# Stick-breaking attention: sums over later keys as split products, with GpSimd making the high part of softplus

## The chip, the cores and the metric

The kernel runs on one core of a Trainium2 chip. The metric is the device time of one launch, in microseconds (us); lower is better. The engines are TensorE (PE in the profile, its weight loads PEld), VectorE (DVE), ScalarE (ACT), GpSimd (POOL) and SyncE (SP), which issues the weight transfers. Each runs its own instructions in order, and they meet at semaphores.

## The reference

Three blocks follow each other on 256 tokens of width 1024. The third has four layers, each a mixer and a squared-ReLU feed-forward part; the mixers of its layers 0 and 3 are stick-breaking attention, with 16 heads of 64:

```
z = einsum('bhqd,bhkd->bhqk', qb, k) * scale
mask = key_pos[None, :] < q_pos[:, None]
log_beta = log_sigmoid(z)
log_1m_beta = where(mask, log_sigmoid(-z), 0.0)
suffix = cumsum(log_1m_beta, axis=3, reverse=True) - log_1m_beta
weights = where(mask, exp(log_beta + suffix), 0.0)
out = einsum('bhqk,bhkd->bhqd', weights, v)
```

With softplus(z) = -log_sigmoid(-z), the exponent is z minus the sum of softplus over this key and all later keys before the query.

## The kernel before

The program is a list of stages (`network`); every engine runs its own part of each stage in turn. All large products of the kernel are split: a weight or a feature x is written as hi + lo, both of type fp32r, where hi is x rounded and lo = x - hi, and three fp32r products replace one fp32 product. ScalarE makes hi of the weights (`in_hi`, line 325) and VectorE makes lo (`in_lo`, line 332).

Keys lie on the partitions, queries in the columns. One step works on a pair of heads. In each head's PSUM bank there are 384 score columns: 256 for the first 128 keys (all queries) and 128 for the last 128 keys (the later queries); so a pair has 768 elements in each partition. `self.e`, `self.sp` and `self.w` are rings of two for |z| and its logarithm, softplus, and weights. `duo` is a ring of three pairs of banks for the scores.

For a pair i the work goes round the engines in this order:

1. TensorE, `_scores`: fp32 products of keys and queries (lines 1629, 1632), and one fp32r product that adds the mask (line 1635).
2. VectorE, `magnitude` (1721): |z|, from PSUM to SBUF.
3. ScalarE: exp(-|z|) and ln(1 + that) (1700, 1701).
4. VectorE, `softplus` (1714): max(z, 0) + that logarithm.
5. TensorE, `_sums` (1643 to 1645): fp32 products of constant matrices of minus one with softplus, added to the scores in the same bank. A fp32 product stands in the trace as two records.
6. ScalarE: the weights, exp of the bank (1692).
7. TensorE, `_values` (1655): fp32 products with the values. ScalarE (1696) and VectorE (1732) then split the result into feat_hi and feat_lo for the output projection.

The eight pairs are pipelined. TensorE's step s is `_scores(s)`, `_sums(s-1)`, `_values(s-2)`. VectorE's step s is `softplus(s-1)`, `magnitude(s)`, then line 1732 for pair s-3. ScalarE's is the weights of s-2, line 1696 for s-3, and lines 1700 and 1701 for s. Steps 0 and 1 stand inside the projection before (`QkvIn`), each after a half of its blocks 4 and 5; there `softplus(0)` comes right before an `in_lo`. Steps 2 to 10 stand in `StickBreaking`. After step LATE = 4 ScalarE and VectorE split one unit of the output projection's weights (`in_hi`, `in_lo`), and `softplus(4)` is behind that `in_lo`. GpSimd has nothing to do in this stage. The output projection (`Linear`, lines 1257 to 1259) begins after the last `_values`.

Of the kernel before, what the change touches and what calls it, by code (L numbers as in the profile page):

```python
# [14 lines left out]
P = 128  # L15
# [121 lines left out]
class Core:  # L137


    def __init__(self, nc, ctx, dram):  # L140
# [49 lines left out]
        self.before_r = placed("before_r", at, F32R, 2, P)  # L190
        self.ident_r = placed("ident_r", at + 4 * 2 * P, F32R, P)
        self.mask_r = placed("mask_r", at + 4 * 3 * P, F32R, 3 * P)
        self.feat2_hi = placed("feat2_hi", at, F32R, KC, TOKENS)
        self.feat2_lo = placed("feat2_lo", at + 4 * KC * TOKENS, F32R, KC, TOKENS)
        self.duo = [ctx.enter_context(nc.psum_tensor(f"duo{i}", [P, 2, 512], F32)) for i in range(4)]
# [90 lines left out]
class Stage:  # L286
# [21 lines left out]
    def gpsimd(self, pool):  # L308
        pass
# [1275 lines left out]
class StickBreaking(Stage):  # L1585
# [12 lines left out]
    def __init__(self, core, before, qT, kT, v, at):  # L1598
        super().__init__(core, before)
        k = core  # L1600
        self.qT, self.kT, self.v = qT, kT, v
        a = k.arena

        def ring(i):
            lo = at + 2 * i * 2 * self.WIDE
            both = a[:, lo:lo + 2 * 2 * self.WIDE].rearrange("p (s h n) -> p s h n", s=2, h=2)
            return [both[:, 0], both[:, 1]]

        self.e, self.sp, self.w = ring(0), ring(1), ring(2)
# [5 lines left out]
        self.c0 = k.sb_consts.plan(2)  # L1615
        self.done = [(k.turn_lo.sem, self.l0 + n)]
        before.sb, self.late = self, before.late

# [19 lines left out]
    def _sums(self, pe, i):  # L1638

        k = self.k  # L1640
        for odd in range(2):
            bank, sp = k.bank[2 * (i % 3) + odd], self.sp[i % 2][:, odd, :]
            pe.matmul(bank[:, 0:256], k.c("minus_tri"), sp[:, 0:256], start=False, stop=False, skip_group_check=True)
            pe.matmul(bank[:, P:256], k.c("minus_ones"), sp[:, 256:384], start=False, stop=False, skip_group_check=True)
            last = pe.matmul(bank[:, 256:384], k.c("minus_tri"), sp[:, 256:384], start=False, stop=True, skip_group_check=True)
        last.then_inc(k.sb_sums.sem, 1)

    def _values(self, pe, i):
# [10 lines left out]
    def step_tensor(self, pe, step):  # L1659
        k, n = self.k, self.n  # L1660
        if step < n:
            if step >= 3:
                pe.wait_ge(k.sb_weights.sem, self.w0 + step - 2)
            self._scores(pe, step)
        if 1 <= step <= n:
            pe.wait_ge(k.sb_softplus.sem, self.sp0 + step)
            self._sums(pe, step - 1)
        if step >= 2:
            pe.wait_ge(k.sb_weights.sem, self.w0 + step - 1)
            if step >= 4:  # L1670
                pe.wait_ge(k.turn_lo.sem, self.l0 + step - 3)
            self._values(pe, step - 2)
# [6 lines left out]
    def prepare(self, act):  # L1679
        k = self.k  # L1680
        act.copy(k.ident_r[:], k.c("ident")).then_inc(k.sb_consts.sem, 1)
        act.copy(k.before_r[:], k.c("beforeadd").unsqueeze(1).broadcast_to([P, 2, P])).then_inc(k.sb_consts.sem, 1)
        act.preload_act_table_set("natural_log_exp_and_others")

    def step_scalar(self, act, step):
# [23 lines left out]
    def softplus(self, dve, i):  # L1709
        k = self.k  # L1710
        dve.wait_ge(k.sb_logs.sem, self.lg0 + i + 1)
        if i >= 2:
            dve.wait_ge(k.sb_sums.sem, self.sum0 + i - 1)
        dve.scalar_tensor_tensor(self.sp[i % 2], self._pair(i), 0.0, self.e[i % 2], ALU.max, ALU.add).then_inc(k.sb_softplus.sem, 1)

    def magnitude(self, dve, i):
        k = self.k
# [5 lines left out]
    def step_vector(self, dve, step):  # L1723
        k, n = self.k, self.n
        if self.EARLY <= step <= n:
            self.softplus(dve, step - 1)
        if step < n:
            self.magnitude(dve, step)
        if step >= 3:
            i = step - 3  # L1730
            dve.wait_ge(k.turn_hi.sem, self.h0 + i + 1)
            dve.tensor_tensor(k.feat_lo[:, i, :], k.bank[6 + i % 2][:, 0:TOKENS], k.feat_hi[:, i, :].bitcast(F32),
                              ALU.subtract).then_inc(k.turn_lo.sem, 1)
# [8 lines left out]
class QkvIn(Linear):  # L1742
# [21 lines left out]
    def block(self, pe, b):  # L1764
# [6 lines left out]
        for h in range(2):  # L1771
# [16 lines left out]
            if h == 0 and b >= 4:  # L1788

                if b == 4:  # L1790
                    pe.wait_ge(k.sb_consts.sem, self.sb.c0 + 2)
                    pe.wait_ge(k.acc_read_dve.sem, self.rd0 + 6)
                self.sb.step_tensor(pe, b - 4)

# [26 lines left out]
    def vector(self, dve):  # L1821
# [4 lines left out]
        for b, (lo, hi) in enumerate(self.blocks):  # L1826
# [14 lines left out]
                                             ALU.mult, ALU.mult).then_inc(k.acc_read_dve.sem, 1)  # L1841
            if b == 4:
                self.sb.softplus(dve, 0)
            if b < 5:
                in_lo(k, dve, self.u0 + 2 * b + 3)

# [196 lines left out]
def more_signals(k):  # L2043
# [19 lines left out]
    k.sb_consts = k.sig("sb_consts")  # L2063
    k.sb_logs = k.sig("sb_logs")
    k.sb_softplus = k.sig("sb_softplus")
    k.sb_sums = k.sig("sb_sums")
    k.gate_copied = k.sig("gate_copied")
    k.gate_turned = k.sig("gate_turned")
# [1570 lines left out]
```

## Time and profile before

| | us |
|---|---|
| median of 3 runs (3110.18 to 3115.7) | 3113.45 |
| profiled execution, own time | 3098.02 |
| span of the profiled execution | 3096.2 |
| TensorE busy | 2828.2 (91%) |
| VectorE busy | 1911.0 (62%) |
| ScalarE busy | 1199.9 (39%) |
| GpSimd busy | 581.0 (19%) |
| mean granted TensorE clock | 0.949 |
| TensorE's share of the chain that ended last | 63% |

Busy time is the union of an engine's instructions; matmuls overlap one another, so a busy TensorE is not one at its peak. A granted clock of 1.00 is 2.4 GHz, 0.50 is 1.2 GHz. The times in the rows below are us from the start of the span, if nothing else is said.

### The profile page before, as it was taken

The page shows a single profiled execution, that of the slowest core. Times are in us where ns is not written, and L with a number is a line of the kernel's source. Part 1 is how long each engine was busy: PE and PEld are TensorE (multiplying, and loading weights), DVE is VectorE, ACT ScalarE, POOL GpSimd, SP SyncE. Part 2 cuts the span into 40 slices and gives each one's busy share as a digit, 9 for nine tenths or more (in the row PEclk, how much of TensorE's full clock was granted, in tenths as well). Part 3 has the DMA queues.
Part 4 walks back from the last instruction along what each step waited for, and adds up shares of the span by engine and source line. Part 5 has one row for each costly group of instructions (what it writes and reads, how often), then busy time and mean ns, then how long its engine had stood idle before and what let it go on. Part 6 is the DMA issues. An engine that isn't in the chain of part 4 may idle for free.

```text
span 3096.2 us, 44930 instructions
## 1 busy us (share of the span) xinstructions
PE 2828.2 (91%) x17998; PEld 2520.2 (81%) x17998; DVE 1911.0 (62%) x2094; ACT 1199.9 (39%) x1427; POOL 581.0 (19%) x477
## 2 busy tenths in 40 slices
PE   8999999999899989895699899998999649999998
PEld 7987799999688879774599778987997548988897
DVE  7876566798669855543555546556654556555554
ACT  4333444333443333341333344334433324334432
POOL 6942200286239600000000000000000010000000
PEclk9999999999999989996799999999999769999999
DMA  7753055576346635340244425435543205434442
GB/s 269 271 193 123 17 211 187 197 255 227 102 170 243 259 131 188 129 136 11 102 183 183 129 86 228 180 131 190 197 187 116 92 7 211 189 118 148 158 189 108
DMA packets 127216, 499.51 MB, mean 161 GB/s; under 512 B 11984, under 2 KB 13296, under 8 KB 93712
## 3 DMA queue, kind: packets, MB, share of 16 engines
q1 hardware_dynamic: 113824, 450.46, 40.0%
q0 software_dynamic: 13296, 47.74, 4.4%
q8 instruction: 64, 1.05, 0.1%
q14 instruction: 32, 0.26, 0.0%
HBM read 497.11 MB, written 1.05 MB: 161 GB/s over the span
## 4 chain that ended last, share of the span: by engine, by line
PE 63%; DVE 16%; issue 12%; ACT 4%; POOL 2%; DMA 2%; DVEq 0%; SPq 0%; POOLq 0%; ACTq 0%
PE duo L943 8%; PE duo L944 8%; PE duo L945 8%; PE duo L1000 5%; PE duo L1002 5%; PE duo L1001 5%; PE duo L1257 5%; PE duo L1259 4%; PE duo L1258 4%; DVE down_lo L332 4%; DVE in_lo L332 3%; ACT in_hi L325 2%; DVE hid_hi L1100 2%; DMA ring_in<-in_ffn_in 2%; POOL arena L1580 1%
## 5 line engine op out<-in xcount | busy, mean ns | idle before, releaser
L943 PE MATMUL duo<-feat_hi,in_hi 128*128 128x256 f32 x3136 | 891.7, 284 | 10.1 <-DVE in_lo L332 6.1
L944 PE MATMUL duo<-feat_lo,in_hi 128*128 128x256 f32 x3136 | 887.7, 283 | 0.0
L945 PE MATMUL duo<-feat_hi,in_lo 128*128 128x256 f32 x3136 | 887.4, 283 | 0.0
L332 DVE TENSOR_TENSOR in_lo<-ring_in,in_hi 128x2048 fp32r<-128x2048 f32 x299 | 712.3, 2383 | 282.8 <-ACT in_hi L325 282.7
L325 ACT CAST in_hi<-ring_in 128x2048 fp32r<-128x2048 f32 (+1 forms) x302 | 571.4, 1892 | 318.8 <-PE duo L1259 235.7
L943 PEld LDWEIGHTS duo<-feat_hi,in_hi 128*128 128x128 f32 x3136 | 602.1, 192 | 23.4 <-DVE in_lo L332 6.5
L944 PEld LDWEIGHTS duo<-feat_lo,in_hi 128*128 128x128 f32 x3136 | 603.4, 192 | 7.3
L945 PEld LDWEIGHTS duo<-feat_hi,in_lo 128*128 128x128 f32 x3136 | 602.6, 192 | 0.0
L332 DVE TENSOR_TENSOR down_lo<-ring_down,down_hi 128x1024 fp32r<-128x1024 f32 (+1 forms) x196 | 371.4, 1895 | 144.3 <-ACT down_hi L325 144.3
L1000 PE MATMUL duo<-down_hi,hid_hi 128*128 128x512 f32 x1040 | 413.2, 397 | 7.7 <-DVE hid_lo L1102 7.4
L1001 PE MATMUL duo<-down_lo,hid_hi 128*128 128x512 f32 x1040 | 410.4, 395 | 0.0
L1002 PE MATMUL duo<-down_hi,hid_lo 128*128 128x512 f32 x1040 | 410.2, 394 | 0.0
L325 ACT CAST down_hi<-ring_down 128x1024 fp32r<-128x1024 f32 (+1 forms) x196 | 259.8, 1326 | 191.2 <-PE duo L1002 190.0
L1257 PE MATMUL duo<-in_hi,feat_hi 128*128 128x512 f32 (+1 forms) x688 | 274.8, 399 | 20.6 <-DVE feat_lo L676 8.1
L1095 DVE TENSOR_TENSOR act<-act,duo 128x256 f32<-128x256 f32 (+1 forms) x196 | 99.6, 508 | 297.1 <-ACT act L1056 252.0
L1258 PE MATMUL duo<-in_lo,feat_hi 128*128 128x512 f32 (+1 forms) x688 | 269.9, 392 | 0.0
L1259 PE MATMUL duo<-in_hi,feat_lo 128*128 128x512 f32 (+1 forms) x688 | 269.6, 392 | 0.0
L1000 PEld LDWEIGHTS duo<-down_hi,hid_hi 128*128 128x128 f32 x1040 | 196.6, 189 | 49.6 <-issue 12.0
L1002 PEld LDWEIGHTS duo<-down_hi,hid_lo 128*128 128x128 f32 x1040 | 196.2, 189 | 46.2
L1001 PEld LDWEIGHTS duo<-down_lo,hid_hi 128*128 128x128 f32 x1040 | 196.4, 189 | 37.3
L1056 ACT ACTIVATE act<-duo 128x512 f32<-128x512 f32 (+1 forms) x108 | 55.4, 513 | 429.0 <-PE duo L945 429.0
L2938 POOL TENSOR_TENSOR mod_sum<-mod_sum,mod_w 128x1024 f32<-128x1024 f32 x63 | 208.0, 3302 | 5.3
(375 smaller groups left out, 3083.3 us busy)
## 6 DMA issues: line engine op xcount, KB each, us to landing
ring_in<-in_ffn_in SPq DMA_DIRECT2D x196, 1024.0 KB, 6.4
ring_down<-in_ffn_down SPq DMA_DIRECT2D x132, 512.0 KB, 3.5
ring_down<-in_ffn_down SPq DMA_DIRECT2D x64, 1024.0 KB, 4.8
mod_w<-in_w_ada POOLq DMA_DIRECT2D x72, 512.0 KB, 5.0
ring_in<-in_sb_w_qkv SPq DMA_DIRECT2D x24, 1024.0 KB, 5.1
ring_in<-in_conv_w_in SPq DMA_DIRECT2D x12, 1024.0 KB, 5.2
ring_in<-in_gla_w_in SPq DMA_DIRECT2D x12, 1024.0 KB, 5.1
ring_in<-in_nsa_w_in SPq DMA_DIRECT2D x10, 1024.0 KB, 5.2
```

Of the source, the lines that this page charges most:

```text
L325: act.copy(hi[:, s, 0:n], raw[:, s, 0:n]).then_inc(hi_ready.sem, 1)
L332: dve.tensor_tensor(lo[:, s, 0:n], raw[:, s, 0:n], hi[:, s, 0:n].bitcast(F32), ALU.subtract).then_inc(lo_ready.sem, 1)
L943: pe.matmul(out, hi, self.feat_hi[:, c, :], start=opens, stop=False, skip_group_check=True)
L944: pe.matmul(out, hi, self.feat_lo[:, c, :], start=False, stop=False, skip_group_check=True)
L945: return pe.matmul(out, lo, self.feat_hi[:, c, :], start=False, stop=(c == KC - 1), skip_group_check=True)
L1000: pe.matmul(out, k.hid_hi[:, j, rows], k.down_hi[:, s, cols], start=opens, stop=False)
L1001: pe.matmul(out, k.hid_hi[:, j, rows], k.down_lo[:, s, cols], start=False, stop=False)
L1002: return pe.matmul(out, k.hid_lo[:, j, rows], k.down_hi[:, s, cols], start=False, stop=closes)
L1257: pe.matmul(out, f_hi, w_hi[:, c, :], start=(h == 0 and c == 0), stop=False)
L1258: pe.matmul(out, f_hi, w_lo[:, c, :], start=False, stop=False)
L1259: last = pe.matmul(out, f_lo, w_hi[:, c, :], start=False, stop=(h == 1 and c == 3))
L2938: pool.tensor_tensor(total, total, mod.w[:, s, :], ALU.add).then_inc(mod.used.sem, 1)
```

## The change

The fp32 products of the sums become two sets of fp32r products, one with the high and one with the low part of softplus. The constant matrices are rounded once into fp32r (minus one and zero are exact). VectorE still writes softplus in fp32; GpSimd copies it into `sp_hi` (fp32r), and VectorE then subtracts that from it to make `sp_lo`. For each pair TensorE does six products on the high part, waits for the low part, and does six on that. VectorE makes the low part of pair s-1 behind `magnitude(s)` of the same step; `softplus(i)` may overwrite its ring as soon as `soft_lo(i-2)` is done, and the two new rings wait for `_sums(i-2)`.

```diff
     def _sums(self, pe, i):
-        for odd in range(2):
-            bank, sp = k.bank[2 * (i % 3) + odd], self.sp[i % 2][:, odd, :]
-            pe.matmul(bank[:, 0:256], k.c("minus_tri"), sp[:, 0:256], start=False, stop=False, ...)
-            pe.matmul(bank[:, P:256], k.c("minus_ones"), sp[:, 256:384], start=False, stop=False, ...)
-            last = pe.matmul(bank[:, 256:384], k.c("minus_tri"), sp[:, 256:384], start=False, stop=True, ...)
+        tri, ones = k.tri_r[:, 0, :], k.tri_r[:, 1, :]
+        pe.wait_ge(k.sb_soft_hi.sem, self.sh0 + i + 1)
+        for part, sp in enumerate((k.sp_hi[:, i % 2], k.sp_lo[:, i % 2])):
+            if part:
+                pe.wait_ge(k.sb_soft_lo.sem, self.sl0 + i + 1)
+            for odd in range(2):
+                bank = k.bank[2 * (i % 3) + odd]
+                pe.matmul(bank[:, 0:256], tri, sp[:, odd, 0:256], start=False, stop=False, ...)
+                pe.matmul(bank[:, P:256], ones, sp[:, odd, 256:384], start=False, stop=False, ...)
+                last = pe.matmul(bank[:, 256:384], tri, sp[:, odd, 256:384], start=False, stop=part == 1, ...)
         last.then_inc(k.sb_sums.sem, 1)
...
     def step_tensor(self, pe, step):
-            pe.wait_ge(k.sb_softplus.sem, self.sp0 + step)
             self._sums(pe, step - 1)
...
     def prepare(self, act):
+        act.copy(k.tri_r[:].rearrange("p i n -> p (i n)"), k.c("minus_tri", 0, 2 * P)).then_inc(k.sb_consts.sem, 1)
...
     def softplus(self, dve, i):
         dve.wait_ge(k.sb_logs.sem, self.lg0 + i + 1)
         if i >= 2:
-            dve.wait_ge(k.sb_sums.sem, self.sum0 + i - 1)
+            dve.wait_ge(k.sb_soft_lo.sem, self.sl0 + i - 1)
         dve.scalar_tensor_tensor(self.sp[i % 2], self._pair(i), 0.0, self.e[i % 2], ALU.max, ALU.add).then_inc(k.sb_softplus.sem, 1)
+
+    def soft_lo(self, dve, i):
+        k = self.k
+        dve.wait_ge(k.sb_soft_hi.sem, self.sh0 + i + 1)
+        if i >= 2:
+            dve.wait_ge(k.sb_sums.sem, self.sum0 + i - 1)
+        dve.tensor_tensor(k.sp_lo[:, i % 2], self.sp[i % 2], k.sp_hi[:, i % 2].bitcast(F32), ALU.subtract).then_inc(k.sb_soft_lo.sem, 1)
+
+    def gpsimd(self, pool):
+        k = self.k
+        for i in range(self.n):
+            pool.wait_ge(k.sb_softplus.sem, self.sp0 + i + 1)
+            if i >= 2:
+                pool.wait_ge(k.sb_sums.sem, self.sum0 + i - 1)
+            pool.tensor_copy(k.sp_hi[:, i % 2], self.sp[i % 2]).then_inc(k.sb_soft_hi.sem, 1)
...
     def step_vector(self, dve, step):
         if self.EARLY <= step <= n:
             self.softplus(dve, step - 1)
         if step < n:
             self.magnitude(dve, step)
+        if self.EARLY <= step <= n:
+            self.soft_lo(dve, step - 1)
...
 class QkvIn(Linear):  # vector(), block 4
             if b == 4:
                 self.sb.softplus(dve, 0)
+                self.sb.soft_lo(dve, 0)
             if b < 5:
                 in_lo(k, dve, self.u0 + 2 * b + 3)
```

The new tiles lie in a part of the arena that the stage didn't use: `sp_hi` and `sp_lo`, [2, 2, 384] each, and `tri_r`, [2, 128].

## Rows read from the trace of the kernel before

**Rows 1.** Busy time by stretch: stretch, its length, then each engine's busy time (and instructions), PEclk, DMA.
```profile
1787.30:1845.20 57.90, 51.97 (x385) 44.66 (x384) 29.11 (x31) 28.89 (x35) 0.00 (x0) 0.94 0.27 91
2820.30:2877.00 56.70, 50.77 (x386) 43.89 (x385) 29.12 (x31) 28.89 (x35) 0.00 (x0) 0.97 0.27 93
...
1826.80:1833.10 6.30, 6.26 (x26) 4.77 (x28) 2.14 (x3) 2.87 (x4) 0.00 (x0) 0.50 0.46 169
...
2859.90:2864.30 4.40, 4.40 (x22) 3.44 (x22) 2.10 (x3) 2.50 (x3) 0.00 (x0) 0.61 0.65 238
```

**Rows 2.** Timeline, steps 2 to 4: start, duration, engine, line, operation, tiles, [idle <-releaser].
```profile
1809.80 0.70 PE L1629 MATMUL duo<-arena 64*128 64x256 f32 x4 [0.88 <-DVE arena L1840]
...
1813.64 0.70 PE L1629 MATMUL duo<-arena 64*128 64x256 f32 x4
...
1813.94 0.96 DVE L1714 SCALAR_TENSOR_TENSOR arena<-duo,arena 128x768 f32<-128x768 f32 x1 [1.78 <-ACT arena L1701]
...
1814.95 0.70 PE L1643 MATMUL duo<-arena,const 128*128 128x256 f32 x2
1815.04 0.96 DVE L1721 TENSOR_SCALAR arena<-duo 128x768 uint32<-128x768 uint32 x1
...
1815.92 0.41 DVE L1732 TENSOR_TENSOR feat_lo<-duo,feat_hi 128x256 fp32r<-128x256 f32 x1
...
1816.03 0.84 ACT L1700 ACTIVATE arena<-arena 128x768 f32<-128x768 f32 x1 [1.16 <-DVE arena L1721]
...
1816.90 0.87 PE L1655 MATMUL duo<-arena,proj 128*64 128x256 f32 x8
...
1817.70 0.70 PE L1629 MATMUL duo<-arena 64*128 64x256 f32 x4
1817.78 0.96 DVE L1714 SCALAR_TENSOR_TENSOR arena<-duo,arena 128x768 f32<-128x768 f32 x1 [1.45 <-ACT arena L1701]
...
1818.90 0.60 PE L1643 MATMUL duo<-arena,const 128*128 128x256 f32 x2
```

**Rows 3.** Timeline of step 5, where the late weight unit is split.
```profile
1821.55 0.70 PE L1629 MATMUL duo<-arena 64*128 64x256 f32 x4
...
1823.63 2.29 DVE L332 TENSOR_TENSOR in_lo<-ring_in,in_hi 128x2048 fp32r<-128x2048 f32 x1 [3.24 <-ACT in_hi L325]
...
1826.84 1.22 PE L1643 MATMUL duo<-arena,const 128*128 128x256 f32 x2 [3.94 <-DVE arena L1714]
...
1830.55 1.55 PE L1655 MATMUL duo<-arena,proj 128*64 128x256 f32 x8
...
1832.03 1.20 PE L1629 MATMUL duo<-arena 64*128 64x256 f32 x4
```

**Rows 4.** Timeline of TensorE: fp32r products that follow each other, at three places.
```profile
1785.02 0.28 PE L1782 MATMUL duo<-feat_hi,in_hi 128*128 128x256 f32 x1
1785.14 0.28 PE L1783 MATMUL duo<-feat_lo,in_hi 128*128 128x256 f32 x1
...
2425.90 0.26 PE L1257 MATMUL duo<-in_hi,feat_hi 128*128 128x16 f32 x1
2426.01 0.26 PE L1258 MATMUL duo<-in_lo,feat_hi 128*128 128x16 f32 x1
...
2432.17 0.36 PE L1258 MATMUL duo<-in_lo,feat_hi 128*128 128x16 f32 x1
2432.38 0.36 PE L1259 MATMUL duo<-in_hi,feat_lo 128*128 128x16 f32 x1
```

**Rows 5.** GpSimd's instructions of two lines: durations in ns, min/median/max, first and last start.
```profile
L2936 POOL TENSOR_SCALAR mod_w<-mod_w,cols x63: 1112/1128/3962, 32.8 to 1049.8; 128x1024 f32<-128x1024 f32 x63
...
L2156 POOL MEMSET arena<- x1: 974/974/974, 223.8 to 223.8; 128x1024 f32 x1
```

**Rows 6.** Timeline of ScalarE and VectorE in the projection before the stage.
```profile
1781.67 1.90 ACT L325 CAST in_hi<-ring_in 128x2048 fp32r<-128x2048 f32 x1 [2.05 <-PE duo L1784]
...
1796.42 2.29 DVE L332 TENSOR_TENSOR in_lo<-ring_in,in_hi 128x2048 fp32r<-128x2048 f32 x1 [0.44 <-ACT in_hi L325]
```

More of the change, by code:

```diff
@@ L192, in __init__ @@
         self.mask_r = placed("mask_r", at + 4 * 3 * P, F32R, 3 * P)
+        self.tri_r = placed("tri_r", at + 4 * 6 * P, F32R, 2, P)
+        self.sp_hi = placed("sp_hi", at - 4 * 2 * 4 * 384, F32R, 2, 2, 384)
+        self.sp_lo = placed("sp_lo", at - 4 * 4 * 384, F32R, 2, 2, 384)
         self.feat2_hi = placed("feat2_hi", at, F32R, KC, TOKENS)
@@ L1614, in __init__ @@
         self.pv0, self.h0, self.l0 = k.sb_valued.plan(n), k.turn_hi.plan(n), k.turn_lo.plan(n)
-        self.c0 = k.sb_consts.plan(2)
+        self.c0 = k.sb_consts.plan(3)
+        self.sh0, self.sl0 = k.sb_soft_hi.plan(n), k.sb_soft_lo.plan(n)
         self.done = [(k.turn_lo.sem, self.l0 + n)]
@@ L1640, in _sums @@
         k = self.k
-        for odd in range(2):
-            bank, sp = k.bank[2 * (i % 3) + odd], self.sp[i % 2][:, odd, :]
-            pe.matmul(bank[:, 0:256], k.c("minus_tri"), sp[:, 0:256], start=False, stop=False, skip_group_check=True)
-            pe.matmul(bank[:, P:256], k.c("minus_ones"), sp[:, 256:384], start=False, stop=False, skip_group_check=True)
-            last = pe.matmul(bank[:, 256:384], k.c("minus_tri"), sp[:, 256:384], start=False, stop=True, skip_group_check=True)
+        tri, ones = k.tri_r[:, 0, :], k.tri_r[:, 1, :]
[5 more added lines that the diff above has]
+                bank = k.bank[2 * (i % 3) + odd]
+                pe.matmul(bank[:, 0:256], tri, sp[:, odd, 0:256], start=False, stop=False, skip_group_check=True)
+                pe.matmul(bank[:, P:256], ones, sp[:, odd, 256:384], start=False, stop=False, skip_group_check=True)
+                last = pe.matmul(bank[:, 256:384], tri, sp[:, odd, 256:384], start=False, stop=part == 1, skip_group_check=True)
         last.then_inc(k.sb_sums.sem, 1)
@@ L1712, in softplus @@
         if i >= 2:
-            dve.wait_ge(k.sb_sums.sem, self.sum0 + i - 1)
-        dve.scalar_tensor_tensor(self.sp[i % 2], self._pair(i), 0.0, self.e[i % 2], ALU.max, ALU.add).then_inc(k.sb_softplus.sem, 1)
+            dve.wait_ge(k.sb_soft_lo.sem, self.sl0 + i - 1)
+        dve.scalar_tensor_tensor(self.sp[i % 2], self._pair(i), 0.0, self.e[i % 2], ALU.max, ALU.add).then_inc(k.sb_softplus.sem, 1)
+    def soft_lo(self, dve, i):
+        k = self.k
+        dve.wait_ge(k.sb_soft_hi.sem, self.sh0 + i + 1)
+        if i >= 2:
+            dve.wait_ge(k.sb_sums.sem, self.sum0 + i - 1)
+        dve.tensor_tensor(k.sp_lo[:, i % 2], self.sp[i % 2], k.sp_hi[:, i % 2].bitcast(F32), ALU.subtract).then_inc(k.sb_soft_lo.sem, 1)
[6 more added lines that the diff above has]
+            pool.tensor_copy(k.sp_hi[:, i % 2], self.sp[i % 2]).then_inc(k.sb_soft_hi.sem, 1)
     def magnitude(self, dve, i):
@@ L1790, in block @@
                 if b == 4:
-                    pe.wait_ge(k.sb_consts.sem, self.sb.c0 + 2)
+                    pe.wait_ge(k.sb_consts.sem, self.sb.c0 + 3)
                     pe.wait_ge(k.acc_read_dve.sem, self.rd0 + 6)
@@ L2065, in more_signals @@
     k.sb_softplus = k.sig("sb_softplus")
+    k.sb_soft_hi = k.sig("sb_soft_hi")
+    k.sb_soft_lo = k.sig("sb_soft_lo")
     k.sb_sums = k.sig("sb_sums")
```

## The prediction

> **What bounds the kernel now.** I read the page first: TensorE is busy 91% of the span and holds 63% of the chain that ended last, so a us saved or lost on TensorE's path counts in full. Next, the busy time by stretch, to see what the change can touch: the two stretches from the first score product to the last value product, 57.90 and 56.70 us, 3.7% of the span; TensorE is busy 51.97 and 50.77 us in them, GpSimd not at all [rows 1]. Last the timeline, step by step.
>
> Steps start with the scores (line 1629): 1809.80, 1813.64, 1817.70 and, in the next group, 1821.55, so steps 2 to 4 take 3.84, 4.06 and 3.85 us [rows 2, 3]. One of 3.85 is TensorE's own work: 1.20 of scores (1817.70 to 1818.90), 1.85 of sums with the switch to the values (3.85 less the other two), 0.80 of values (1816.90 to 1817.70). The step of 4.06 shows how little slack is left: there the sums wait for softplus and start at 1814.95, not 1814.84. So in this stretch two limits lie side by side: TensorE's work, 3.85, and the round from one pair's scores to its softplus.
>
> Step 5 differs: softplus(4) stands behind the late weight unit's in_lo (1823.63, 2.29 us), TensorE is idle 3.94 us, and then works at half clock: 0.50 from 1826.80 to 1833.10; in the second layer the same place has 0.61 over 4.40 us [rows 1, 3]. Step 5 takes 10.48 us (1821.55 to 1832.03).
>
> **TensorE's own saving.** There are 16 pairs in all (8 in each of two layers). A pair's sums take 1.75 us without the switch. The new ones are four fp32r products of 256 columns and eight of 128. An fp32r product of 256 columns takes 0.12 us (1785.02 to 1785.14). One of 128 is not in the trace; one of 16 takes 0.11 (2425.90 to 2426.01), so the loading of 128 weight columns is what is paid, and 128 columns lie between 0.11 and 0.12 [rows 4]. I take 0.112: 4 x 0.120 + 8 x 0.112 = 1.38 us, 0.69 for each part. Saved: 0.37 a pair, 6.0 us for 16, if TensorE never waits. At half clock the narrow ones take 0.21 (2432.17 to 2432.38), so about 2.57 against twice 1.75.
>
> The Trainium skill (TensorE: Matmul & The Clock Gate, Back-to-back issue gap) gives an isolated product of 128 columns N/2.4 + 2.5 ns, 56 ns; by that a part takes 0.44 instead of 0.69, and the forecast would be about 3 us lower. The row of 16 columns at 0.11 us speaks for the other pace, that of the weight load.
>
> **What the sums wait for now.** The order on VectorE is softplus(s-1), magnitude(s), soft_lo(s-1). Magnitude(s) reads the scores that TensorE makes in this same step, so the low part can't be ready before them. From the start T of the scores:
> - magnitude(s) starts at T + 1.40 (1813.64 to 1815.04), and the next VectorE instruction 0.88 later (1815.92) [rows 2];
> - soft_lo(s-1) starts at T + 2.28. It is a subtraction of 768 elements; VectorE's others of that length take 0.96 [rows 2], the one of 2048 takes 2.29 [rows 3], 0.86 by proportion. I take 0.95;
> - 0.05 to TensorE (softplus ends at 1814.90, sums start 1814.95), 0.11 for weights that are now loaded in the open (that group of two products takes 0.70, the unstalled one at 1818.90 takes 0.60) [rows 2];
> - so the low products start at T + 3.39, take 0.69, then 0.10 of switch and 0.80 of values: the next scores at T + 4.98.
>
> The high products (0.69 from T + 1.20) lie inside this wait. A steady step is thus 4.98 us: TensorE idles some 1.3 us in it and gains nothing from its shorter products. Against 3.85 that is +1.13.
>
> **GpSimd's copy.** The trace has no such copy. Its nearest rows: a one-input instruction of 1024 columns takes 1.112 at least and 3.96 at most, a memset 0.97 [rows 5]. For 768 columns that is 0.83 to 2.97, and 0.73 by the memset. The low ones are instructions that nothing disturbed, and here VectorE runs magnitude (which reads PSUM) or waits; I take 0.88. In a steady step: exp starts 0.99 after magnitude(s) (1815.04 to 1816.03), softplus 1.75 after exp (1817.78), it lasts 0.96, so softplus(s) ends at T + 5.10, which is the next scores' T + 0.12; copied by T + 1.06 with 0.06 for the handoff. The high products want it at T + 1.20, soft_lo at T + 2.28: the copy is hidden, and would be up to about 2 us. Not at three places of each layer, where it is paid in full: step 2, step 5 and the last sums.
>
> The Trainium skill (GPSIMD Engine Reference, section 3.1) puts a one-input loop between 1.03 and 1.8 cycles an element at 1.2 GHz; at 1.8 it would be 1.15 us plus dispatch, some 2 us more over the six places. No row here shows a copy at that pace.
>
> **The sum, per layer.**
> - Step 1, inside the projection: softplus(0) and both parts are ready long before, so 0.37 saved.
> - Steps 2 to 4: 5.08 (softplus(1) is late there, by 0.1) + 4.98 + 4.98 = 15.04 against 11.75: +3.29.
> - Step 5: the late unit's split now begins some 1.1 us earlier after the scores, for ScalarE is ahead of the slower TensorE. Softplus(4) ends near T + 4.1, copied T + 5.1, low part T + 6.05. High products at half clock 1.3 from T + 5.2, low ones 1.3, values 1.48 (1830.55 to 1832.03 [rows 3]): 9.4 to 9.8, I take 9.6. Against 10.48: -0.9. In the second layer, with less time at half clock before, -0.4.
> - Step 6: +1.2 (+1.1 in the second).
> - After the last scores: from the end of softplus(7) to the end of its sums it was 0.05 + 0.11 + 1.75; now 0.06 + 0.88 + 0.03 + 0.95 + 0.05 + 0.11 + 0.69: +0.9.
>
> First layer +4.1, second +4.5: +8.6 us. At nothing I cost: the copy of the constants on ScalarE (0.4 by its neighbours' length, in a place where ScalarE then idles 2.05 us), and soft_lo(0) before an in_lo (starts 1796.42, ends 1798.71, would end 1.4 later; TensorE takes that unit up only behind step 1's scores and sums, 2.6 us of its work) [rows 6]; if that cover were gone it would cost under 2 us a layer. After the stage the weights are split ahead as before; nothing is given back.
>
> 3098.02 + 8.6 = 3106.6 for the profiled execution. The median of the runs shown is 15.4 us above that execution, and I carry the difference over: 3113.45 + 8.6 = **3122**.
>
> **Rivals.**
> 1. *The low part is never late*, and TensorE's shorter work decides: 16 x 0.37 = 6.0 saved, and about 0.5 more in each stretch at half clock: 3106 to 3107. For it: where TensorE is the last to arrive (step 1, half clock) it is so, and two limits were almost equal before. It decides if the wait is under 0.37 a step, which needs soft_lo ready 1.0 us sooner than the rows give. If half is recovered the time doesn't change. 0.14.
> 2. *The clock falls*: TensorE now idles in each step, its products are narrow, and after step 5 it may stay at 1.2 GHz. A step at half clock: magnitude about T + 2.6, low products T + 4.6, 1.3, 0.1, 1.5: 7.5, +2.5. Three such stretches a layer (steps 6, 7 and the tail) are +7: 3129 in one layer, 3136 in both. Against it: TensorE still works 3.6 of each 4.98 us, and before it came back within 6.3 us. 0.14.
> 3. *GpSimd is slow*, at 2.97 as in its most disturbed row: 2.1 us more at six places, and up to 1 in the others' steps: 3134; at 1.4, 3125. 0.07.
> 4. *Narrow fp32r products are paid like fp32 ones*, 0.22 for 128 columns: a part takes 1.12, and +0.43 at seven places a layer: 3128. No row excludes it, since 16 columns can hide behind the weight load. 0.05.
>
> My own case has 0.60.
>
> **How the numbers follow.** The forecast's own range is 3118 to 3126. Below 3110 only rival 1 lies, above 3135 only the ends of 2 and 3; so 3110 to 3135. About 0.2% (6.2 us) is what a measurement of this kernel can tell from no change. My case is centred 2.4 us beyond that: 0.40 slower, 0.20 same. Rivals 2, 3 and 4 are slower: 0.26. Rival 1: 0.07 faster, 0.07 same. Sum: faster 0.07, same 0.27, slower 0.66.
>
> **What would show it.** In the changed timeline: score starts 5.0 us apart in steps 2 to 4, TensorE waiting for VectorE's new subtraction between the two sets of products, 1.2 to 1.4 us each time; fp32r products of 128 columns 0.11 apart; GpSimd's eight copies a layer near 0.9 us; the two stretches 62.0 and 61.2 us long. Steps of 3.9 or less would refute it, and so would high products that start late, since then the copy and not VectorE's order decides.

## The result, and the profile after

| 20 runs each | us |
|---|---|
| kernel before, median (lowest to highest) | 3106.28 (3099.88 to 3115.7) |
| changed kernel, median (lowest to highest) | 3119.7 (3109.86 to 3125.22) |
| ratio, 95% interval | 1.0038 [1.0027, 1.0049] |
| the same in us, on 3106.28 | +11.8 [+8.4, +15.2] |
| profiled execution of the changed kernel | 3124.35 (span 3122.5) |

The change is slower, by more than the 0.2% that this kernel's measurement can tell from nothing. The forecast was +8.6 us, just above the lower end of the interval.

The spans of the two profiled executions differ by 26.3 us, more than twice the measured difference. Part of that lies ahead of the stage: the first score product of step 2 comes at 1809.80 before [rows 2] and at 1820.32 after, though the code up to there differs only in the first pair's sums, which gain 0.39 us. Single executions of either kernel spread over 15 us. So I compare the two stretches, not the spans. First the busy time by stretch in the changed kernel; the columns are those of [rows 1]. The first two rows are the stretches from the first score product to the output projection, the third is steps 2 to 4 of the first layer, the fourth its steps 6, 7 and the last sums, the fifth steps 2 and 3 of the second layer.

```profile
1798.20:1862.10 63.90, 52.03 (x385) 44.41 (x384) 36.15 (x39) 29.78 (x35) 7.17 (x9) 0.90 0.28 90
2839.90:2903.10 63.20, 51.63 (x387) 44.40 (x385) 36.14 (x39) 29.79 (x35) 7.17 (x9) 0.92 0.28 91
1820.30:1835.00 14.70, 11.19 (x90) 8.99 (x90) 8.79 (x11) 8.20 (x11) 2.48 (x3) 1.00 0.00 1
1844.40:1862.10 17.70, 13.97 (x90) 10.44 (x88) 7.95 (x11) 7.29 (x11) 2.21 (x3) 0.79 0.09 30
2862.10:2873.40 11.30, 9.09 (x62) 7.05 (x62) 6.46 (x8) 5.29 (x7) 1.65 (x2) 0.85 0.01 1
```

Two things are to be seen. The stretches have grown from 57.90 and 56.70 us [rows 1] to 63.90 and 63.20, while TensorE is busy for nearly as long as before (51.97 and 50.77 then, 52.03 and 51.63 now): the added time is idle time of TensorE. Equal busy time is not equal work, though: the sums are cheaper now, and more of the work runs at half clock. For the granted clock fell from 0.94 and 0.97 to 0.90 and 0.92. To the hundredth, the stretches sum to 114.63 us before and 127.10 after: +12.5 us, which is the measured +11.8 within its interval.

The length of each step, from its first score product to the next step's (the last entry, step 7 and the last sums and values, ends at the output projection), as it can be read from the starts of TensorE's groups of scores:

```
              step 0   1     2     3     4     5      6     7+end   sum
before,   L1  12.81  9.73  3.84  4.06  3.84  10.48  4.33   8.87   57.97
before,   L2  12.81  9.73  3.84  4.06  3.85   9.66  3.84   8.87   56.66
changed,  L1  12.81  9.34  4.90  4.90  4.90   9.36  6.25  11.51   63.98
changed,  L2  12.81  9.34  5.34  5.92  4.90   9.24  5.92   9.64   63.12
```

L1 and L2 are the first and the second stick-breaking layer. Step 3 of the first layer in the changed kernel, start, duration, engine, line, operation and tiles as in [rows 2]; line 1633 is the scores, 1652 to 1654 the new sums, 1664 the values, 1738 GpSimd's copy, 1745 magnitude, 1730 the low part, 1723 softplus:

```profile
1825.23 0.70 PE L1633 MATMUL duo<-arena 64*128 64x256 f32 x4
1825.48 0.83 POOL L1738 CAST sp_hi<-arena 128x768 fp32r<-128x768 f32 x1 [3.55 <-DVE arena L1723]
1826.36 0.19 PEld L1652 LDWEIGHTS duo<-sp_hi,tri_r 128*128 128x128 f32 x1
1826.42 0.33 PE L1652 MATMUL duo<-sp_hi,tri_r 128*128 128x256 f32 x1
1826.47 0.19 PEld L1653 LDWEIGHTS duo<-sp_hi,tri_r 128*128 128x128 f32 x1
1826.58 0.22 PE L1653 MATMUL duo<-sp_hi,tri_r 128*128 128x128 f32 x1
1826.59 0.19 PEld L1654 LDWEIGHTS duo<-sp_hi,tri_r 128*128 128x128 f32 x1
1826.62 0.96 DVE L1745 TENSOR_SCALAR arena<-duo 128x768 uint32<-128x768 uint32 x1 [1.21 <-PE duo L1639]
1826.64 0.27 PE L1654 MATMUL duo<-sp_hi,tri_r 128*128 128x128 f32 x1
...
1827.50 0.95 DVE L1730 TENSOR_TENSOR sp_lo<-arena,sp_hi 128x768 fp32r<-128x768 f32 x1
...
1828.50 0.39 PE L1652 MATMUL duo<-sp_lo,tri_r 128*128 128x256 f32 x1 [1.24 <-DVE sp_lo L1730]
...
1829.33 0.87 PE L1664 MATMUL duo<-arena,proj 128*64 128x256 f32 x8
1829.37 0.96 DVE L1723 SCALAR_TENSOR_TENSOR arena<-duo,arena 128x768 f32<-128x768 f32 x1 [0.59 <-ACT arena L1710]
...
1830.13 0.49 PE L1633 MATMUL duo<-arena 64*128 64x256 f32 x2
```

With T = 1825.23 as the start of the scores, magnitude starts at T + 1.39, the low part at T + 2.27, the low products at T + 3.27, the values at T + 4.10, the next scores at T + 4.90. The high products start at T + 1.19, 0.11 us after the copy ends, so the copy is not late here. TensorE then waits 1.24 us for the low part. Last, the durations of the two new instructions over all 16 pairs (ns, min/median/max):

```profile
L1738 POOL CAST sp_hi<-arena x16: 826/827/827, 1806.9 to 2898.6; 128x768 fp32r<-128x768 f32 x16
...
L1730 DVE TENSOR_TENSOR sp_lo<-arena,sp_hi x16: 946/948/960, 1807.8 to 2899.5; 128x768 fp32r<-128x768 f32 x16
```

### The profile page after: what moved, and what is told of

Read it like the earlier page. It is cut to its first block, busy times and chain, and to the rows that moved or that the text cites. A ratio compares the mean times of both kernels' runs of the same rounds, so it can differ in the third digit from the quotient of the medians.

```text
span 3122.5 us, 44988 instructions
## 1 busy us (share of the span) xinstructions
PE 2836.1 (91%) x17998; PEld 2526.9 (81%) x17998; DVE 1926.0 (62%) x2110; ACT 1202.6 (39%) x1429; POOL 594.1 (19%) x493
## 4 chain that ended last, share of the span: by engine, by line
PE 62%; DVE 15%; issue 14%; ACT 4%; POOL 3%; DMA 2%; DVEq 0%; SPq 0%; POOLq 0%; ACTq 0%
PE duo L946 8%; PE duo L947 8%; PE duo L948 8%; PE duo L1003 5%; PE duo L1004 5%; PE duo L1005 5%; PE duo L1260 5%; PE duo L1261 5%; PE duo L1262 4%; DVE down_lo L335 3%; DVE in_lo L335 2%; DVE hid_hi L1103 2%; ACT in_hi L328 2%; DMA ring_in<-in_ffn_in 2%; POOL arena L1583 1%
## 5 line engine op out<-in xcount | busy, mean ns | idle before, releaser
L946 PE MATMUL duo<-feat_hi,in_hi 128*128 128x256 f32 x3136 | 891.5, 284 | 13.4 <-DVE in_lo L335 7.3
L946 PEld LDWEIGHTS duo<-feat_hi,in_hi 128*128 128x128 f32 x3136 | 602.2, 192 | 27.3 <-DVE in_lo L335 7.4
L1003 PE MATMUL duo<-down_hi,hid_hi 128*128 128x512 f32 x1040 | 413.6, 398 | 10.3 <-DVE hid_lo L1105 10.1
```

The source lines that it names most:

```text
L946: pe.matmul(out, hi, self.feat_hi[:, c, :], start=opens, stop=False, skip_group_check=True)
L1003: pe.matmul(out, k.hid_hi[:, j, rows], k.down_hi[:, s, cols], start=opens, stop=False)
```

## The experiments

My theory: VectorE's order (the low part behind the magnitude, which reads this step's scores) sets the step, and TensorE, idle in it, also loses clock. The rivals were that the copy on GpSimd is what is late, and that the steps' growth is all there is and the clock is incidental. Each ratio is to the kernel before, with its 95% interval. e1 to e4 were timed on one chip, beside 17 runs of the kernel before, and e5 to e8 on another, beside 30.

### Other orders

**e1_lo_first.** The low part before the magnitude on VectorE:

```diff
-        if step < n:
-            self.magnitude(dve, step)
         if self.EARLY <= step <= n:
             self.soft_lo(dve, step - 1)
+        if step < n:
+            self.magnitude(dve, step)
```

> VectorE makes the low part of pair s-1 in front of magnitude(s) instead of behind it. If it mattered only that the low part stands behind the magnitude (rival), TensorE's wait falls to about 0.2 us and a step to 4.0 us or less, the kernel comes down to the time of before (ratio 0.999 to 1.001 against before). By my theory, two rounds of dependent work share VectorE: now magnitude waits for GpSimd's copy and for the low part, softplus to softplus is 0.06 + 0.83 + 0.03 + 0.88 + 0.99 + 1.75 + 0.96, about 5.5 us, so steps 3 and 4 take 5.4 to 5.6 us instead of 4.90, each layer is about 4 to 5 us longer than with the change, ratio 1.006 to 1.008.

Measured: 1.0064 [1.0045, 1.0082] (3126.1 against 3105.42), stretches of 66.34 and 66.44 us. The timeline of its step 3:

```profile
1828.56 0.96 DVE L1723 SCALAR_TENSOR_TENSOR arena<-duo,arena 128x768 f32<-128x768 f32 x1 [1.78 <-ACT arena L1710]
...
1829.58 0.83 POOL L1738 CAST sp_hi<-arena 128x768 fp32r<-128x768 f32 x1 [4.67 <-DVE arena L1723]
1830.44 0.96 DVE L1730 TENSOR_TENSOR sp_lo<-arena,sp_hi 128x768 fp32r<-128x768 f32 x1 [0.92 <-POOL sp_hi L1738]
1830.46 0.38 PE L1652 MATMUL duo<-sp_hi,tri_r 128*128 128x256 f32 x1 [1.52 <-POOL sp_hi L1738]
...
1831.32 0.95 DVE L1745 TENSOR_SCALAR arena<-duo 128x768 uint32<-128x768 uint32 x1
...
1832.30 0.84 ACT L1709 ACTIVATE arena<-arena 128x768 f32<-128x768 f32 x1 [2.81 <-DVE arena L1745]
...
1834.05 0.96 DVE L1723 SCALAR_TENSOR_TENSOR arena<-duo,arena 128x768 f32<-128x768 f32 x1 [1.45 <-ACT arena L1710]
```

Now one ring runs through every instruction of the pair: softplus, the copy (VectorE idles 0.92 us for it), the low part, the magnitude, exp, ln, softplus: 5.49 us (1828.56 to 1834.05). TensorE no longer waits for the low part, but 1.52 us for the high part, and the loop is longer than 4.90. So by the stretches (132.78 us in sum for 127.10) the order of the change is the better of the two, and neither order is free. Some of the difference is the clock again: 41.4 us of these two stretches are at half clock, where the changed kernel has 23.1. The steps themselves alternate (4.28, 6.51, 4.49 for steps 2 to 4) instead of settling at 5.4 to 5.6, which I had not foreseen; the sum of steps 3 and 4 is 11.0, two rounds of 5.5.

**e2_values_first.** TensorE's step becomes scores(s), values(s-2), sums(s-1), so that the values' 0.80 us stand in the wait for the low part:

```diff
-        if 1 <= step <= n:
-            self._sums(pe, step - 1)
         if step >= 2:
             ...
             self._values(pe, step - 2)
+        if 1 <= step <= n:
+            self._sums(pe, step - 1)
```

> TensorE's step is scores(s), values(s-2), sums(s-1): the 0.9 us of values stand inside the wait for the low part. My theory: the low products still start 3.4 us after the scores, then 0.8 to the next scores, steps of 4.1 to 4.2 us instead of 4.90; each layer about 3.6 us shorter at full clock, ratio 1.000 to 1.002 against before, and fewer stretches at half clock than with the change. If GpSimd's copy were what bounds the step (rival), the order on TensorE would change nothing: steps stay at 4.9, ratio 1.004.

Measured: steps 2 to 4 take 4.10, 4.10, 4.10 in both layers, 0.80 less than in the changed kernel: the wait is 0.29 us and not 1.24 in the timeline of its step 3.

```profile
1824.22 0.70 PE L1633 MATMUL duo<-arena 64*128 64x256 f32 x4
...
1825.51 0.87 PE L1664 MATMUL duo<-arena,proj 128*64 128x256 f32 x8
...
1827.50 0.39 PE L1652 MATMUL duo<-sp_lo,tri_r 128*128 128x256 f32 x1 [0.29 <-DVE sp_lo L1730]
...
1828.33 0.49 PE L1633 MATMUL duo<-arena 64*128 64x256 f32 x2
```

That confirms the wait: all of the values' 0.80 us fitted into it. But the ratio is 1.0054 [1.0035, 1.0072], where 1.000 to 1.002 was expected: a miss, no gain on the changed kernel (1.0038) shows. The row of its first stretch says where it went:

```profile
1798.00:1861.60 63.60, 56.36 (x386) 47.79 (x385) 36.17 (x39) 29.13 (x35) 7.17 (x9) 0.82 0.26 91
```

The clock in it is 0.82. TensorE fell to half clock in step 5 and stayed there for 27.3 us: steps 5 to the end take 8.39, 6.54 and 14.19, where the changed kernel has 9.36, 6.25 and 11.51. Of the three steps' gain of 2.4 us, 2.0 are given back by the end of the stretch, and more behind it, for the half clock lasts 4.6 us into the output projection:

```profile
1862.99 0.63 PE L1260 MATMUL duo<-in_hi,feat_hi 128*128 128x512 f32 x1
...
1866.52 0.39 PE L1260 MATMUL duo<-in_hi,feat_hi 128*128 128x512 f32 x1
```

From the projection's first product to the fifth of line 1260 (the row at 1866.52) it is 4.97 us here and 3.25 in the changed kernel. The second layer's stretch is 59.95 us long, 3.2 less than in the changed kernel, but there too 4.1 us at half clock follow behind it. Counted to that fifth product, the two layers are 12.93 us longer than before in this kernel and 12.88 in the changed one: the order gained nothing in all. This was the first sign that the clock is a term of its own here, of the size of the effect under study.

**e3_no_lo_wait.** The second six products read the high part again and wait for nothing; the low part is left out of the sums (VectorE still makes it):

```diff
-        for part, sp in enumerate((k.sp_hi[:, i % 2], k.sp_lo[:, i % 2])):
-            if part:
-                pe.wait_ge(k.sb_soft_lo.sem, self.sl0 + i + 1)
+        for part, sp in enumerate((k.sp_hi[:, i % 2], k.sp_hi[:, i % 2])):
```

> The second six products read the high part again and don't wait for the low part; VectorE still makes it (the low part is left out of the sums). TensorE's work is that of the change, the wait for VectorE is gone, the copy by GpSimd stays. My theory: steps of 4.0 to 4.4 us (the round through GpSimd's copy, 8.4 us for two steps, decides with TensorE's 3.6), each layer 3.4 us shorter than with the change, ratio about 1.001. If the copy were the cause (rival), steps stay near 4.9.

Measured: 1.0019 [1.0007, 1.0031]. Steps 2 to 4 fall from 4.90 each to 3.97, 4.38, 3.97, so in the first layer the wait for the low part is worth 2.4 us in these three. Yet they are not shorter than before (3.84, 4.06, 3.85), though the products are. The timeline of step 4 shows what is late next:

```profile
1820.62 0.96 DVE L1721 SCALAR_TENSOR_TENSOR arena<-duo,arena 128x768 f32<-128x768 f32 x1 [0.59 <-ACT arena L1708]
...
1820.86 0.70 PE L1633 MATMUL duo<-arena 64*128 64x256 f32 x4
...
1821.64 0.83 POOL L1736 CAST sp_hi<-arena 128x768 fp32r<-128x768 f32 x1 [3.15 <-DVE arena L1721]
...
1822.53 0.38 PE L1650 MATMUL duo<-sp_hi,tri_r 128*128 128x256 f32 x1 [0.31 <-POOL sp_hi L1736]
```

(L1721 is softplus and L1736 the copy in this kernel.) Softplus of the pair ends 0.7 us after the scores start, the copy adds 0.83 and a handoff, and TensorE waits 0.31 for the high part, 0.71 in step 3. So even with no low part the round, which was level with TensorE's work before, is longer by the copy. Two steps make one round, since the scores of step s+2 stand behind the sums of pair s: steps 3 and 4 together took 7.90 us before and take 8.35 now. From the end of softplus to the high products it is 0.95 us instead of 0.05 [rows 2], 0.90 more, and the cheaper sums take about 0.4 off the round. In a steady step the link costs more than the cheaper products save.

### The copy on another engine

**e8_copy_by_vector.** VectorE makes the high part itself, right behind softplus; GpSimd has nothing to do in the stage:

```diff
+    def soft_hi(self, dve, i):
+        ...
+        dve.tensor_copy(k.sp_hi[:, i % 2], self.sp[i % 2]).then_inc(k.sb_soft_hi.sem, 1)
...
-    def gpsimd(self, pool):
-        ...
             self.softplus(dve, step - 1)
+            self.soft_hi(dve, step - 1)
         if step < n:
```

> VectorE makes the high part too, right behind softplus; GpSimd does nothing in the stage. An fp32 copy of 768 elements from SBUF to SBUF on VectorE is not in the trace; I take 0.5 to 0.96 us. If GpSimd's copy were in the way (rival), steps get shorter than 4.90. By my theory the copy was hidden in a steady step and now stands in front of magnitude only as far as scores come later: softplus(s-1) ends at about T + 0.1, the copy at T + 0.6 to T + 1.1, magnitude starts at T + 1.40 as before: steps 3 and 4 stay at 4.90, and the places where the copy was paid (step 2, step 5, the last sums) are the same or up to 0.4 us shorter each: ratio 1.003 to 1.004.

Measured: 1.0042 [1.0024, 1.006], no different from the changed kernel. The timeline of its step 3:

```profile
1816.11 0.56 DVE L1730 CAST sp_hi<-arena 128x768 fp32r<-128x768 f32 x1
...
1819.16 0.39 PE L1652 MATMUL duo<-sp_lo,tri_r 128*128 128x256 f32 x1 [1.29 <-DVE sp_lo L1737]
```

The copy takes VectorE 0.56 us where GpSimd takes 0.83, ends earlier, and the step is still 4.90, with the same wait for the low part (1.29 for 1.24). That rules GpSimd out: the copy's length and engine do not set the steady step. Step 5 is 9.52 us in both layers, 0.16 and 0.28 longer than with GpSimd, where the same or less was expected: the copy now stands ahead of the magnitude and the low part on VectorE, whose subtraction starts 5.57 us after the scores and not 5.11 (first layer).

### The clock

Four kernels fill TensorE's idle time with unused fp32r products: ones of 128 weights by 256 columns, of finite constants, into PSUM columns (256 to 511 of the values' banks) that the stage neither reads nor writes otherwise. They change nothing of the result.

```diff
+    def _warm(self, pe, i, count):
+        k = self.k
+        for _ in range(count):
+            pe.matmul(k.bank[6 + (i + 1) % 2][:, 256:512], k.ident_r[:], k.before_r[:].rearrange("p i n -> p (i n)"), start=False, stop=False, skip_group_check=True)
```

**e4_filled.** The changed kernel with ten of them in each low part's wait of steps 3 to 7:

```diff
             if part:
+                if self.EARLY < i + 1 < self.n:
+                    self._warm(pe, i, 10)
                 pe.wait_ge(k.sb_soft_lo.sem, self.sl0 + i + 1)
```

> The change plus ten unused fp32r products of 256 columns (1.2 us) between the high and the low products of pairs 1 to 6, into PSUM columns that nobody reads. At full clock they lie inside the wait of 1.3 us: steps 3 and 4 stay at 4.90 to 4.95. If part of the change's loss (about 4 of 12.5 us) is TensorE at half clock after step 5, because it is less busy, the clock is back to 1.00 after one stretch as before and the two layers are together 3 to 4 us shorter than with the change: ratio 1.0025 to 1.003. If the clock has no part in it (rival), nothing changes: 1.004, or it is slower by what the products cost at half clock.

(The edit fills the waits of pairs 2 to 6, not of pair 1.) Measured: 1.0045 [1.0029, 1.006], not less than the changed kernel. A miss: I had left the long wait of step 5 open, the clock fell there as before, and the ten products then ran at half clock in step 5 (11.15 us and not 9.36 in the first layer). The time at half clock in the two stretches went from 23.1 to 15.6 us, and the fill ate what that gave. Steps 2 and 3 of the second layer, where step 2's wait was left open, are as long as in the changed kernel (5.37 and 5.92).

**e5_before_filled.** The kernel before, with 32 of them in step 5 ahead of the wait for softplus(4), where it idles 3.94 us [rows 3]:

```diff
+            if step == self.LATE + 1:
+                pe.wait_ge(k.turn_lo.sem, self.l0 + step - 3)
+                self._warm(pe, step - 1, 32)
             pe.wait_ge(k.sb_softplus.sem, self.sp0 + step)
             self._sums(pe, step - 1)
```

> The kernel before, plus 32 unused fp32r products of 256 columns (3.84 us) between scores(5) and the wait for softplus(4), where TensorE idles 3.94 us. If that idling is what puts TensorE at half clock in steps 5 and 6, the clock stays at 1.00, step 5 takes 8.1 us instead of 10.48 and 9.66, step 6 3.85: the two layers are 4.4 us shorter, ratio 0.9985. If the clock falls anyway (rival), the products cost up to their length at half clock: ratio 1.000 to 1.001.

Measured: 0.9981 [0.9969, 0.9992] (3101.04 against 3106.9), as expected. Its two stretches:

```profile
1793.50:1848.60 55.10, 52.98 (x418) 46.52 (x417) 29.12 (x31) 28.66 (x35) 0.00 (x0) 1.00 0.29 95
2825.00:2880.10 55.10, 52.99 (x418) 46.54 (x417) 29.12 (x31) 28.65 (x35) 0.00 (x0) 1.00 0.28 95
```

And step 5, which has 4 us of unused work in it and is 2.4 us shorter (8.06 for 10.48):

```profile
1827.81 0.70 PE L1629 MATMUL duo<-arena 64*128 64x256 f32 x4
...
1829.00 3.99 PE L1652 MATMUL duo<-before_r,ident_r 128*128 128x256 f32 x32
...
1832.11 0.95 DVE L1723 SCALAR_TENSOR_TENSOR arena<-duo,arena 128x768 f32<-128x768 f32 x1
...
1833.11 0.70 PE L1643 MATMUL duo<-arena,const 128*128 128x256 f32 x2
...
1835.06 0.87 PE L1661 MATMUL duo<-arena,proj 128*64 128x256 f32 x8
...
1835.86 0.49 PE L1629 MATMUL duo<-arena 64*128 64x256 f32 x2
```

Softplus(4) comes no sooner; what follows runs at 2.4 GHz: the sums start 5.30 us after the scores in both kernels (1826.84 less 1821.55 before), and from there to the next scores it is 2.75 us instead of 5.19. The two stretches are 110.11 us where the kernel before has 114.63: half clock cost it 4.5 us. This kernel has the lowest median of all here.

**e6_all_filled.** The changed kernel with 30 in step 5 and ten in every other low part's wait from step 2 to the last sums:

```diff
             if part:
+                if self.EARLY <= i + 1 <= self.n and i != self.LATE:
+                    ...
+                    self._warm(pe, i, 10)
                 pe.wait_ge(k.sb_soft_lo.sem, self.sl0 + i + 1)
...
+            if step == self.LATE + 1:
+                pe.wait_ge(k.turn_lo.sem, self.l0 + step - 3)
+                self._warm(pe, step - 1, 30)
             self._sums(pe, step - 1)
```

> The change, with 30 such products before the high products of pair 4 and ten in each wait for a low part (pairs 1 to 3 and 5 to 7). If the clock stays at 1.00, what is left is the price of the order alone: steps 2 to 4 at 4.90, step 5 7.8, step 6 4.9, tail 9.9, 59.6 us a layer against 57.97 and 56.66 before: +4.6 us, ratio 1.0015; the change itself had +12.5 in these stretches, so some 8 us of it would be the clock's. If the clock plays no part, 1.004 again.

Measured: 1.0016 [1.0007, 1.0026], as expected; steps 12.81, 9.34, 5.17, 4.90, 4.91, 7.75, 4.90, 10.53 in both layers, 60.32 us each.

```profile
1794.90:1855.20 60.30, 57.56 (x476) 51.45 (x475) 36.16 (x39) 29.82 (x35) 7.19 (x9) 1.00 0.29 96
```

The clock is 1.00 with the steps' order untouched, and the ratio is 0.22% lower than the changed kernel's (1.0016 against 1.0038, two sets of runs; e8, with TensorE's steps as in the change and timed beside e6, has 1.0042); the stretches say 127.10 less 120.64, 6.5 us. The clock of whole executions, as the median over the timed runs, goes the same way: 0.946 in the changed kernel and 0.941 in e2, where the kernel before has 0.949 beside e1 to e4; 0.948 in the kernel before and 0.9485 to 0.9495 in e5, e6 and e7 in the other set. With e5, this shows the clock to be a cause and not a companion. In two places the fill overshoots its wait: step 2 has 5.17 and not 4.90, and the tail 10.53, where the changed kernel's second layer, at full clock there, has 9.64. The row below, of the last sums, shows it: 1.40 us of fill in a wait that was under 0.3 (in the changed kernel the last low products start 0.99 us after the high ones, which take 0.73).

```profile
1851.43 1.40 PE L1665 MATMUL duo<-before_r,ident_r 128*128 128x256 f32 x10
1852.67 0.28 PE L1656 MATMUL duo<-sp_lo,tri_r 128*128 128x256 f32 x1
```

**e7_values_first_filled.** e2's order with 30 in step 5 and four in each other low part's wait:

> TensorE's order scores(s), values(s-2), sums(s-1), with 30 products in step 5 and four in each wait for a low part. Steps of 4.1 us as without the products; with the clock at 1.00 step 5 7.8, step 6 4.1, tail 9.9: 56.1 us a layer against 57.97 and 56.66, ratio 0.9990 to 0.9995, faster than the change by 0.4 to 0.5%. If the clock falls all the same, 1.003 or more, as the same order without the products (1.0054).

Its edit is those of e2 and e6 together, with a 4 in place of the 10 and without e6's extra wait in the low part's fill. Measured: 0.9988 [0.9975, 1.0], as expected; steps 2 to 4 at 4.10, step 5 8.46, step 6 4.10, the tail 9.81, 56.82 us in both layers, at full clock:

```profile
1802.80:1859.60 56.80, 52.81 (x439) 47.12 (x438) 36.16 (x39) 29.17 (x35) 7.17 (x9) 1.00 0.30 102
```

With the wait mostly used and the clock held, the split sums are at 56.82 a layer where the fp32 sums with the same care are at 55.06 (e5): they still lose 1.8 us a layer. That the whole is not slower than the kernel before (the interval ends at 1.0, the stretches say 1.0 us less) is because that one loses 4.5 us to the clock.

### All of them together

The sum of the two stretches less 114.63, as a share of 3106; the same with both stretches carried on to the fifth product of line 1260 (1257 in the kernel before and in e5), where all kernels are back at full clock; and the measured ratio:

```
                          stretches, us  by them   carried on   measured
changed                        127.10    1.0040    1.0041   1.0038 [1.0027, 1.0049]
e1_lo_first                    132.78    1.0058    1.0063   1.0064 [1.0045, 1.0082]
e2_values_first                123.52    1.0029    1.0042   1.0054 [1.0035, 1.0072]
e3_no_lo_wait                  119.69    1.0016    1.0016   1.0019 [1.0007, 1.0031]
e4_filled                      126.28    1.0038    1.0040   1.0045 [1.0029, 1.006]
e5_before_filled               110.11    0.9985    0.9985   0.9981 [0.9969, 0.9992]
e6_all_filled                  120.64    1.0019    1.0019   1.0016 [1.0007, 1.0026]
e7_values_first_filled         113.64    0.9997    0.9997   0.9988 [0.9975, 1.0]
e8_copy_by_vector              126.00    1.0037    1.0037   1.0042 [1.0024, 1.006]
```

By the stretches alone e2 lies outside its interval; carried on until its half clock has ended, all nine lie inside. So the two stretches, with the half clock that outlasts them, account for the measured effects as far as the intervals can tell.

## Why the prediction was right, and where it was off

**The order of VectorE** set the step, as the prediction said: scores 4.90 us apart in steps 2 to 4 of the first layer (4.98 forecast), a wait of 1.24 us for the subtraction (1.2 to 1.4), every event of the chain within 0.02 us up to the end of the subtraction. From the subtraction's end to the values it is 0.88 us (1828.45 to 1829.33) for 0.95: the weight load in the open costs 0.05 and not 0.11, since the six low products of this step have 0.73 with it in the open (and 0.10 of switch behind them), where six that wait for nothing take 0.68 (e3's second six: 1823.26 to 1824.03 less the switch, 0.67). e2 and e3 moved or removed that wait and the steps followed, e8 moved the copy and they did not. The rival in which the low part is never late fell with them.

**TensorE's saving** came where nothing was waited for: step 1 is 0.39 us shorter (0.37 forecast), in both layers. Narrow fp32r products are not paid like fp32 ones, at 0.22, so that rival fell too. The weight loads of the six high products follow each other by 0.10 to 0.12 us (the first three at 1826.36, 1826.47 and 1826.59), whether 128 or 256 columns are multiplied, and the six take 0.68 where the prediction had 0.69: that is the loads' pace. The Trainium skill's rule for isolated products (TensorE: Matmul & The Clock Gate, Back-to-back issue gap; 56 ns for 128 columns) is met by the trace only between two neighbours of 128 columns (1826.58 to 1826.64). It doesn't give the six; the same section warns that the formula under-counts at small widths in a stream where each product has a weight load.

**GpSimd's copy**: 0.827 us in all 16 pairs, for 0.88 taken and 0.73 to 2.97 as bounds; hidden in steps 3 and 4, paid in step 2 (0.31 us of wait), step 5 and the last sums. The slow case of it didn't happen. Durations on GpSimd are rough in a profile, but TensorE's 0.90 us more between softplus and the high products (e3) bears this one out. The Trainium skill (GPSIMD Engine Reference, section 3.1) has 1.03 to 1.8 cycles an element: 0.827 us is 1.29 cycles of 1.2 GHz with all fixed costs in it, in the lower half.

**Step 5** was 9.36 and 9.24 (9.6 forecast). As forecast, the late unit's split starts earlier after the scores (1836.05 for scores at 1835.03), and softplus(4) ends at T + 4.18 (4.1 forecast). **The last sums** cost 0.77 (9.64 less 8.87 where both are at full clock) for 0.9. Term by term, us against the kernel before:

```
                        forecast        measured
                        L1     L2       L1     L2
step 1                 -0.4   -0.4     -0.4   -0.4
steps 2 to 4           +3.3   +3.3     +3.0   +4.4
step 5                 -0.9   -0.4     -1.1   -0.4
step 6                 +1.2   +1.1     +1.9   +2.1
step 7 and the end     +0.9   +0.9     +2.6   +0.8
sum                    +4.1   +4.5     +6.0   +6.5
```

The four terms that came out well above the forecast (steps 2 to 4 of the second layer, step 6 of both, the end of the first) are the ones in which TensorE ran at half clock where it hadn't before, or for longer.

**The term that was mis-sized is the clock.** The prediction had the stage's clock lose only what it lost before, step 5, and gave 0.14 to a case in which it falls further. It does, in part: half clock covers 23.1 us of the two stretches, 10.2 before, by the granted clock of the records (from the windows' rounded column, twice one less PEclk by the length, it is 22.9 and 10.3). In the first layer it comes back at 1845.9, falls again for the values and scores at 1849.3 and for the last values at 1859.6, as the timeline's durations show (the columns as before):

```profile
1844.39 1.23 PE L1633 MATMUL duo<-arena 64*128 64x256 f32 x4
...
1846.31 0.28 PE L1652 MATMUL duo<-sp_hi,tri_r 128*128 128x256 f32 x1
...
1849.21 1.49 PE L1664 MATMUL duo<-arena,proj 128*64 128x256 f32 x8
1850.63 1.23 PE L1633 MATMUL duo<-arena 64*128 64x256 f32 x4
...
1859.45 2.77 PE L1664 MATMUL duo<-arena,proj 128*64 128x256 f32 x16
1862.15 0.80 PE L1260 MATMUL duo<-in_hi,feat_hi 128*128 128x512 f32 x1
```

Scores' groups of 1.23 us beside the 0.70 of full clock, the last values 2.77 beside 1.84. In the second layer it fell in step 2 already, which the prediction had excluded by leaving steps 2 to 4 alone. TensorE had waited ahead of each fall: 3.77 us in step 5, 1.28 in step 6, 1.07 ahead of the last sums, 0.31 and 0.71 in step 2 of the second layer. But a wait alone does not tell of a fall: steps 3 and 4 of the first layer have 1.24 and 1.23, and no fall.

The sizes come from e6 and e5. e6 holds the clock and has the change's order: 120.64, less 2.3 of overshoot (0.27 + 0.89, twice), is 118.3 us. Against the changed kernel's 127.1 that leaves 8.8 us for its half clock; the kernel before loses 4.5 (e5). So:

```
order, copy and saving at full clock   118.3 - 110.1 = +8.2
half clock, 8.8 now for 4.5 before                    +4.3
sum                                    127.1 - 114.6 = +12.5   (measured +11.8 [8.4, 15.2])
```

The split into +8.2 and +4.3 is an inference, since the overshoot is subtracted by two step lengths and not by a run without it, and it rests on one profiled execution of each kernel, in which the falls differ even from layer to layer. The forecast's +8.6 was a sum with the old clock in it, so it is the +8.2 that it met; the further half clock, which the prediction's second rival had priced at 14 us for both layers, came at about a third of that. The forecast time of 3122 holds a second difference: it was carried to a median of 3113.45, and in the longer series the kernel before has 3106.28. The profiled execution lies 8.3 us below that median, not the 15.4 that the prediction carried over. The base came out 7.2 us lower and the effect, by the medians, 4.8 higher (13.4 for 8.6); so the time's closeness to 3119.7 is in part luck, two errors of opposite sign.

What stays open: what decides a fall and a return, as why e2, with less waiting than the changed kernel (7.3 us for 11.8 from step 2 of the first layer on), stayed at half clock for 27 us without a break, and the changed kernel came back after 6.8. No run here varies the kind of work at a constant idle time.

## What to carry to other kernels

- A part that two products need (high and low) doubles the deadlines, not only the work: find the later one's place in its engine's order, and ask whether what stands ahead of it waits for the consumer's own present step. Here the magnitude did, and 1.24 us of idle time a step bought nothing.
- Where the chain is already level with the busiest engine, a further link that makes this engine's work cheaper pays in a steady step only if the link is shorter than what it saves. Here it was 0.90 us against 0.39, so the saving showed only where TensorE is last to arrive (0.39 us in step 1).
- Where TensorE idles for a few us and the trace shows half clock behind it, unused products in the wait are worth a try before anything else: on the kernel before they gave 0.19% [0.08, 0.31]. They must fit the wait, and they must cover the place where the clock falls, not one behind it (e4 against e6).
- When stretches of two kernels are compared, carry them on until the granted clock is the same again. e2's stretches ended inside its half clock and hid 4 us of its cost.

## What the runs showed of the hardware that was not expected

- A fill of 4 us of unused products made a step 2.4 us shorter (e5), for all of the work behind it ran at 2.4 GHz and not at 1.2.
- The clock also fell where TensorE waited no more than 0.9 us at a time: in step 2 of the second layer, whose waits were 0.31 and 0.71 us after 0.88 at its start (granted clock 0.85 over 2862.1 to 2873.4), while the same step of the first layer, with the same waits, kept 1.00.
- Converting 768 columns from fp32 to fp32r in SBUF takes VectorE 0.56 us and GpSimd 0.83, while VectorE's subtraction of two such operands takes 0.95.
- A step order with less idle time in steps 2 to 4 (e2) ended with the lowest clock of all, 0.82 over its first stretch and 0.941 as the median of its whole executions.
